# One hybrid decoder layer: token rows gathered in fp32 at 48 seats per expert, and 4 MB of expert 16 loaded before the expert loop

## What is computed

```python
exp_logits = ((xt @ w_expert).astype(jnp.float32) + b_expert.astype(jnp.float32)
              ).reshape(-1, N_GROUPS, EXPERTS_PER_GROUP)
sel_logits = jnp.take_along_axis(exp_logits, grp_idx[:, :, None], axis=1)[:, 0]
top_p, top_idx = lax.top_k(jax.nn.softmax(sel_logits, axis=-1), TOP_K)
...
for e in range(N_EXPERTS):
    he = jax.nn.silu(xt @ w1[e]) * (xt @ w3[e])
    y = y + combine[:, e:e + 1] * (he @ w2[e]).astype(jnp.float32)
```

## Time and profile before

| | us |
|---|---|
| median of 3 runs | 1478.21 |
| lowest, highest | 1477.36, 1479.08 |
| profiled execution, device time | 1476.32 |
| its span (first to last instruction) | 1474.5 |

### The profile page before, as it was taken

How to read it: one execution, slowest core, us unless ns; L and a number is a source line. 1 busy time by engine, 2 the same in 40 slices (tenths; PEclk the granted TensorE clock), 3 DMA queues, 4 the chain that set the end, 5 groups by cost and what they waited for, 6 DMA issues and landing times.

```text
span 1474.5 us, 20318 instructions
## 1 busy us (share of the span) xinstructions
PE 1355.0 (92%) x7740; PEld 834.6 (57%) x7740; DVE 612.2 (42%) x1136; ACT 440.0 (30%) x865; POOL 65.1 (4%) x63
## 2 busy tenths in 40 slices
PE   5999999999999798899999999899899889899885
PEld 3899999999988653343353353353353344335332
DVE  5977787778864611232223212212222122222223
ACT  5465655656654411111021011111111111111102
POOL 0012221022100000000000000000000000000000
PEclk9999999999999999999999999999999999999998
DMA  7565555555546759999999999999999999999994
GB/s 204 151 156 151 147 148 151 128 149 144 200 143 212 309 230 430 426 428 428 427 428 429 428 428 428 429 425 425 428 429 428 428 429 428 427 428 429 428 428 173
DMA packets 147064, 481.63 MB, mean 327 GB/s; under 512 B 11385, under 2 KB 112978, under 8 KB 121810
## 3 DMA queue, kind: packets, MB, share of 16 engines
q1 hardware_dynamic: 147026, 481.10, 83.5%
HBM read 478.96 MB, written 2.12 MB: 326 GB/s over the span
## 4 chain that ended last, share of the span: by engine, by line
PE 67%; DMA 24%; DVE 5%; ACT 2%; issue 1%; SPq 1%; DVEq 0%; ACTq 0%
PE bank L562 65%; DMA ew<-in_expert_w_dram 23%; PE bank L565 2%; DVE w_parts L1430 1%; ACT ew L1342 1%; DMA mixT<-in_x_dram 1%; SPq L529 0%; ACT fw_r L1269 0%; DVE ew L1469 0%; DVE fw L1889 0%; ACT fw L1009 0%; DVE fw_r L1750 0%; DVE fw L1390 0%; DVE fw L1940 0%; DVE ew L1897 0%
## 5 line engine op out<-in xcount | busy, mean ns | idle before, releaser
L562 PE MATMUL bank<-ew,hT 128*64 128x512 f32 (+1 forms) x1568 | 466.7, 602 | 39.5 <-DMA ew<-in_expert_w_dram 32.0
L562 PEld LDWEIGHTS bank<-ew,hT 128*64 128x64 f32 (+1 forms) x1568 | 157.1, 141 | 336.1 <-issue 335.9
L562 PE MATMUL bank<-act_parts,w_parts 128*128 128x256 f32 x2304 | 308.1, 288 | 1.7 <-DVE w_parts L1430 1.7
L562 PEld LDWEIGHTS bank<-act_parts,w_parts 128*128 128x128 f32 x2304 | 285.2, 191 | 2.9 <-issue 1.4
L562 PE MATMUL bank<-ew 128*64 128x512 f32 (+2 forms) x1120 | 248.8, 574 | 6.8 <-DVE ew L1899 6.8
L562 PE MATMUL bank<-mixT,hT 128*64 128x512 f32 x512 | 227.0, 596 | 0.0
L1897 DVE SCALAR_TENSOR_TENSOR ew<-ew,bank 128x256 f32<-128x256 f32 x32 | 13.5, 421 | 453.9 <-ACT ew L1344 453.9
L562 PEld LDWEIGHTS bank<-ew 128*64 128x64 f32 (+1 forms) x1120 | 84.8, 141 | 147.5 <-issue 137.2
L1430 DVE TENSOR_TENSOR w_parts<-fw,w_parts 128x2048 fp32r<-128x2048 f32 x64 | 147.8, 2313 | 31.5 <-ACT w_parts L1031 30.5
L1359 ACT ACTIVATE ye_r<-bank 64x512 fp32r<-64x512 f32 x128 | 68.8, 585 | 279.7 <-PE bank L562 278.9
L1342 ACT ACTIVATE ew<-bank,gs 128x512 f32<-128x512 f32 x32 | 22.0, 687 | 422.1 <-PE bank L562 422.1
(11 more groups left out here) (243 smaller groups left out, 1084.3 us busy)
## 6 DMA issues: line engine op xcount, KB each, us to landing
ew<-in_expert_w_dram SPq DMA_DIRECT2D x160, 2048.0 KB, 16.2
mixT<-in_expert_w_dram SPq DMA_DIRECT2D x32, 2048.0 KB, 18.6
fw<-in_w_in_dram SPq DMA_DIRECT2D x48, 1024.0 KB, 5.9
fw<-in_w_out_dram SPq DMA_DIRECT2D x16, 1024.0 KB, 5.0
mixT<-in_x_dram SPq DMA_DIRECT2D x1, 2048.0 KB, 7.4
fw<-in_x_dram SPq DMA_DIRECT2D x1, 2048.0 KB, 9.7
out_dram<-fw SPq DMA_DIRECT2D x4, 512.0 KB, 2.7
hT<-decay_rows SPq DMA_DIRECT2D x8, 192.0 KB, 5.8
```

Source lines behind the costliest of these rows:

```text
L562: return nc.tensor.matmul(o, l, r, start=start, stop=stop, skip_group_check=True)
```

## The change

**Gather.** The row split is gone. The gather reads the fp32 residual `x2` itself through a view (`xk`) whose 128 channels of a block lie 16 floats (64 bytes) apart, with 48 columns per expert: 16 x 2 = 32 fp32 products of 192 columns. The gathered rows lie in `seats`, 48 per expert; the up products still load 64 columns of it (the last only 48). Rounds would be needed from 49 tokens per expert on, before from 65. The one-hot columns beyond 48 are zeroed once by GpSimd. The first gather is cut 4 + 4 groups instead of 5 + 3, and expert j=0 waits for the gathered groups one by one. The experts' outputs are added into a copy `acc` of the residual, which ACT makes in four copies (`keep`), because `x2` is now read by every gather.

**Ahead.** Pieces 0 and 1 of expert 16 are loaded before the loop into four spare places (2 MB, 1 MB, 0.5 MB, 0.5 MB); in the loop SP skips these two loads, and the loop is written in two parts around expert 16.

**Order on PE.** The first half of `combine` moves ahead of the transposes of j=0 and j=2, and the gate columns ahead of those of j=3; DVE's additions move likewise. The router's weights and some small tiles move to other places.

```diff
-def build(nc, ins, out, slots=SLOTS):
+def build(nc, ins, out, slots=SEATS):
...
+        spare = sb("spare", [P, 1024])
+        R6 = Region(spare[:, :], 1024)
...
-        hn_hi = [fw_r[:, D:2 * D], fw_r[:, 2 * D:3 * D]]
-        hn_lo = [misc_r[:, 0:D], fw_r[:, 0:D]]
+        acc = fw[:, 0:2 * D].rearrange("p (t d) -> p t d", t=NT)
+        xk = x2.rearrange("q t (p k) -> q t k p", k=KD)
+        seats = hT[:, :, :].rearrange("p a b -> p (a b)")
+        XT = KD * QUAD * SEATS
+        ahead = [fw[:, 2 * D:4 * D], misc[:, 0:D], spare[:, :], seats[:, XT:XT + 1024]]
...
+        wfin = fw[:, 4 * D:5 * D]
+        rw = cst[:, C_BIG:C_BIG + KD * 36].rearrange("p (k n) -> p k n", k=KD)
+        rb = cst[:, C_BIG + KD * 36:C_BIG + KD * 36 + 36]
...
-                    sp.wait_ge(s_proj, NH * 6 + 7)
+                    sp.wait_ge(s_atm, NH * (LEVELS - 1))
+                    sp.wait_ge(s_aq, NH)
...
             load_expert(0, 0)
             load_expert(0, 1)
+            sp.wait_ge(s_y, NH)
+            sp.wait_ge(s_mix, 2 * NH)
+            sp.dma_start(ahead[1], expert_piece(AHEAD, 1)[:, 0:D]).then_inc(s_ahead, 16)
+            sp.dma_start(ahead[2], expert_piece(AHEAD, 1)[:, D:D + 1024]).then_inc(s_ahead, 16)
+            sp.wait_ge(s_proj, NH * 6 + 8)
+            sp.wait_ge(s_restD, NH * 6 + 15)
+            sp.dma_start(ahead[0], expert_piece(AHEAD, 0)).then_inc(s_ahead, 16)
             for piece in range(2, 6):
                 sp.wait_ge(s_proj, NH * 6 + min(12 + piece, 16))
                 load_expert(0, piece)
+            sp.wait_ge(s_lgt, NT)
+            sp.dma_start(ahead[3], expert_piece(AHEAD, 1)[:, D + 1024:]).then_inc(s_ahead, 16)
...
             with sp.Fori(0, rounds) as r:
-                with sp.Fori(1, NE) as e:
+                with sp.Fori(1, AHEAD) as e:
+                    for piece in range(6):
+                        sp.wait_ge(s_ed, (r * NE + e - 1) * 6 + piece + 1)
+                        load_expert(e, piece)
+                for piece in range(2):
+                    sp.wait_ge(s_ed, (r * NE + AHEAD - 1) * 6 + piece + 1)
+                    sp.nop().then_inc(s_ew[piece], 16)
+                for piece in range(2, 6):
+                    sp.wait_ge(s_ed, (r * NE + AHEAD - 1) * 6 + piece + 1)
+                    load_expert(AHEAD, piece)
+                with sp.Fori(AHEAD + 1, NE) as e:
                     for piece in range(6):
                         sp.wait_ge(s_ed, (r * NE + e - 1) * 6 + piece + 1)
                         load_expert(e, piece)
...
@@ -858,18 +888,15 @@
             mm(bank[5][:, 2 * NE:3 * NE], one, hot[:, 0:NE], True, False)
             mm(bank[5][:, 2 * NE:3 * NE], one, hot[:, NE:], False, True).then_inc(s_rank, 1)
 
...
-            pe.wait_ge(s_hnH, 2 * NT)
-            pe.wait_ge(s_hnL, 2 * NT)
...
+            seated = pick[:, :, :, 0:P].rearrange("p t a (b s) -> p t a b s", s=SLOTS)[:, :, :, :, 0:SEATS]
 
             def gather_group(o, g):
                 for c in range(2):
-                    for lo in range(2):
-                        for t in range(NT):
-                            k = 2 * g + c
-                            l = mm(o[:, c * T:(c + 1) * T], (hn_lo if lo else hn_hi)[t][:, k * P:(k + 1) * P],
-                                   pickr[:, t, :, 0:P], lo == 0 and t == 0, lo == 1 and t == NT - 1)
+                    for t in range(NT):
+                        l = mm(o[:, c * WIDE:(c + 1) * WIDE], xk[:, t, 2 * g + c, :], seated[:, t], t == 0, t == NT - 1)
                 l.then_inc(s_xg, 1)
...
+                pe.wait_ge(s_pz, 1)
                 pe.wait_ge(s_pick, n + 1)
                 pe.wait_ge(s_turn, r + 1)
-                for g in range(5):
+                for g in range(4):
                     gather_group(bank[FIRST[g]], g)
...
-                for g in range(5, 8):
+                for g in range(4, 8):
                     if g == 6:
                         pe.wait_ge(s_xeA, n * 4 + 1)
-                    else:
+                    elif g > 4:
                         pe.wait_ge(s_xeD, n * 4 + (1 if g == 5 else 2))
                     gather_group(bank[FIRST[g]], g)
                 pe.wait_ge(s_gq0, 1)
                 gate_slots()
 
-            def gather_next(n):
+            def gates_next(n):
 
                 pe.wait_ge(s_pick, n + 1)
                 for t in range(NT):
                     pe.wait_ge(s_add[t], n * 8 - 4)
                 gate_slots()
...
+            def gather_next(n):
+
                 for g in range(8):
                     if g >= 2:
                         pe.wait_ge(s_xeA if g % 2 else s_xeD, n * 4 + g // 2)
...
-            def combine(n, pair):
+            def combine(n, pair, t):
 
                 m = pe.snap(n * 2 + pair)
-                pe.wait_ge(s_placeT, n + 1)
-                pe.wait_ge(s_yeA, m * 8 + 8)
-                pe.wait_ge(s_yeD, m * 2 + 2)
-                for i in range(8):
+                if t == 0:
+                    pe.wait_ge(s_placeT, n + 1)
+                    pe.wait_ge(s_yeA, m * 8 + 8)
+                    pe.wait_ge(s_yeD, m * 2 + 2)
+                for i in range(t * 4, t * 4 + 4):
...
+            def quad(n, q, first, last, has_ahead=False):
...
-                        if j == 0:
-                            pe.wait_ge(s_xeA, n * 4 + 2 + 2 * half)
-                            pe.wait_ge(s_xeD, n * 4 + 2 + 2 * half)
                         for which in range(2):
                             pe.wait_ge(s_ew[half * 2 + which], e * 16 + 16)
+                        if has_ahead and j == 0 and half == 0:
+                            pe.wait_ge(s_ahead, 64)
                         for k in range(KD // 2):
+                            if j == 0 and k % 2 == 0:
+                                pe.wait_ge(s_xeA if k % 4 else s_xeD, n * 4 + 2 * half + k // 4 + 1)
+                            at = (half * 8 + k) * WIDE + j * SEATS
+                            rows = min(SLOTS, XT - at)
                             for which in range(2):
-                                l = mm(bank[2][which * 64:which * 64 + 64, :],
-                                       xT[:, half * 8 + k, j * SLOTS:(j + 1) * SLOTS],
-                                       ewp[half * 2 + which].rearrange("p (k n) -> p k n", n=FF)[:, k, :],
+                                l = mm(bank[2][which * 64:which * 64 + rows, :], seats[:, at:at + rows],
+                                       up_weights(half * 2 + which, k, has_ahead and j == 0),
                                        half == 0 and k == 0, half == 1 and k == KD // 2 - 1)
                                 if k == KD // 2 - 1:
...
+                    if j == 0 and not first:
+                        combine(pe.snap(n - 1), 1, 0)
+                    elif j == 2:
+                        combine(n, 0, 0)
+                    elif j == 3 and not last:
+                        gates_next(pe.snap(n + 1))
                     pe.wait_ge(s_hs, e + 1)
                     for k in range(FC):
                         l = tr(bank[3][:, k * P:(k + 1) * P], hs.rearrange("p (f k) -> p k f", k=FC)[:, k])
                     l.then_inc(s_HT, 1)
                     if j == 0 and not first:
-                        combine(pe.snap(n - 1), 1)
+                        combine(pe.snap(n - 1), 1, 1)
                     if j == 1:
                         places(n, first)
                     if j == 2:
-                        combine(n, 0)
+                        combine(n, 0, 1)
                     if j == 3 and not last:
                         gather_next(pe.snap(n + 1))
...
-                with pe.Fori(1, NQUAD - 1) as q:
+                with pe.Fori(1, AHEAD // QUAD) as q:
+                    quad(pe.snap(r * NQUAD + q), q, False, False)
+                quad(pe.snap(r * NQUAD + AHEAD // QUAD), AHEAD // QUAD, False, False, True)
+                with pe.Fori(AHEAD // QUAD + 1, NQUAD - 1) as q:
                     quad(pe.snap(r * NQUAD + q), q, False, False)
                 quad(pe.snap(r * NQUAD + (NQUAD - 1)), NQUAD - 1, False, True)
-                combine(pe.snap(r * NQUAD + (NQUAD - 1)), 1)
+                for t in range(NT):
+                    combine(pe.snap(r * NQUAD + (NQUAD - 1)), 1, t)
...
-            def high_rows(t, lo, hi):
-                act.activation(hn_hi[t].rearrange("q (k p) -> q k p", k=KD)[:, :, lo:hi],
-                               x2[:, t].rearrange("q (p k) -> q k p", k=KD)[:, :, lo:hi], ACT.Copy).then_inc(s_hnH, 1)
-
+            def keep(t, lo, hi):
+                act.activation(acc[:, t, lo:hi], x2[:, t, lo:hi], ACT.Copy)
...
-            act.wait_ge(s_restD, NH * 6 + 15)
-            high_rows(1, 0, 96)
+            act.wait_ge(s_restD, NH * 6 + 16)
+            for t in range(NT):
+                keep(t, 0, 3 * 512)
...
-                        l = act.activation(xT[:, 2 * g + c, :], bank[banks[g]][:, c * T:(c + 1) * T], ACT.Copy,
```

(36 more changed lines are left out.)

70 lines of the change are left out of this document (32 added, 38 removed).

## The result

| | us |
|---|---|
| kernel before, median of 4 runs beside it | 1477.78 |
| changed kernel, median of 4 runs | 1506.03 (1503.25 to 1508.53) |
| ratio, with its 95% interval | 1.0194 (1.018 to 1.0209) |
| profiled execution of the changed kernel, its span | 1508.53, 1506.7 |

The change costs 28 us. The forecast was no change, 1478 us, with a range of 1473 to 1500: the measured 1506 lies outside it. What the prediction called rival 1 (the stationary load at a 64-byte stride) is the mechanism, at a higher price than it was given.

What follows compares the result with a forecast made beforehand. The DMA queue was taken as the bound, so time is stream start, bytes and tail. Terms -9.8 + 6.8 + 2.6 - 0.5 = -0.9, plus 0.9 for lower clock: no change, 1478 us, range 1473 to 1500.

Steps and rivals of the forecast that it cites:

- rival 1: Gather's stationary load at a 64-byte stride: 0.21 to 0.225 us an instruction, +14 to +25 us, near 1496; chance 0.27.
- The gather: Each expert gather: 64 fp32 instructions at 0.16 to 0.17 us, 10.3 to 10.9 us against 8.6, +2.3, mostly covered.
- six quads: Under rival 1, gathers in six other quads: DMA queue idles 0.7 + 0.5, lower clock 1 to 2 more; 1.2 to 3 each.
- The hole: DMA queue near expert 16, short of two preloaded pieces: idle 6.3 us, then 0.5 before expert 17's piece 0; +6.8.
- The first gather: Expert 0's gather, before the unbroken stream: nothing covers it, 12.3 us with the lower clock against 9.7; +2.6.
- Ahead of the loop: Path to the round count: row split removed, partly offset by short compares and smaller one-hot writes; -0.5 us.
- the order around the transposes: PE at three places in a quad: 3.5 to 4 us more slack, none in the time while the queue is the bound.
- loads ahead of the loop: Expert 16's two pieces leave the stream, -9.8 us; loading them in idle DMA time before the loop costs nothing.

Runs made afterwards that it cites:

- the first probe: Changed kernel plus 128 extra fp32 products, results overwritten, at strides of 1 to 32 floats ahead of the gather for experts 16 to 19; no kernel time given.

## Why the prediction was wrong

**The step that failed first is "The gather".** "The floor set by loading 128 stationary columns is 1.87/16 = 0.117, which lies beneath 0.16": that row was of a contiguous load. At the 64-byte stride the load takes 0.21 to 0.22, and the columns (0.164, as worked out) vanish beneath it. The two bounds were both in the text, and the choice between them went by the wrong row: the `hs` transposes are PE's own and at a stride of 16 bytes, but they are transposes, and those do not pay. The rows of ACT and DVE, given less weight because they were other engines, said 1.8 to 1.9, and it was 0.222/0.117 = 1.9. The rule that the prediction quotes from the Trainium skill (SBUF — State Buffer, Specifications) was right for this load, and I weighed it down by a row of another operation.

**The price of rival 1 (+14 to +25) was too low**, mainly in one term: six quads at 1.2 to 3 us, which lost 2.3 to 5.1. Its hole, 6.8 + 3.6 = 10.4, was 12.6, and the tail's 1.6 was not in it; its first gather, +6.2, was right (+6.1). Two things are in the quads. Its formula had 13.5 + 14.2 = 27.7 against a queue of 27.9, so nearly no gap. But a queue that is nearly dry is slower already: behind the gather shown above the transfer is at 240 GB/s for 3 us though its share is 0.75, and once more when the next piece pair starts:

```profile
767.00:770.00 3.00, 3.00 (x18) 1.00 (x15) 0.00 (x0) 0.00 (x0) 0.00 (x0) 1.00 0.75 240
...
779.00:781.00 2.00, 2.00 (x12) 0.60 (x10) 0.00 (x0) 0.00 (x0) 0.00 (x0) 1.00 0.88 262
```

That is 1.3 + 0.8 us of this gather's 2.3. And in three of the six quads the lower clock fell on half 1 ahead of the gather, which delayed piece 4 by some 1.7 more (8.8 for 7.1, as in the tail):

```profile
860.00:865.00 5.00, 3.54 (x10) 1.34 (x12) 0.00 (x0) 0.00 (x0) 0.00 (x0) 0.70 1.02 436
```

Those three lost 4.0 to 5.1, the others 2.3 to 2.7.

**The hole (+6.8)** was right in kind and too small. With the gather as assumed it is 9.8: of it 6.2 behind the gather (991 to 998, predicted 6.3), but 2.0 more ahead of pieces 2 and 3 (979 to 982). Half 1 took 8.8 us at the lower clock, and the queue holds only 8.3 then; I had taken 7.1 and seen no gap. The rest is the slow return to rate. (The prediction's own last part, 3.5 + 7.1 less 9.8, is 0.8 and not 0.5.) With the 14.2 us gather the hole is 12.6. Of that an ordinary gather would have lost 2 to 5 anyway, so the two pieces' 9.8 us were lost, and no more than that.

**The first gather (+2.6)** is 15.8 - 9.7 = +6.1 with the stride, and 7.8 + 5.3 = 13.1 without, +3.4: the lower clock cost 2.6 where I took 1.7. **Ahead of the loop (-0.5)**: the gather starts at 516.07 against 515.69, so no gain shows; but between the traces of the variants without extra products it starts anywhere from 515.02 to 516.29, so 0.5 us can't be told.

**Right:** that the queue bounds the loop and the ledger is to be made from its start, bytes and idling; that 64 instructions at their columns' pace take 10.3 to 10.9 (10.49); that the order around the transposes brings 3.5 to 4 us of slack per quad (3.6) and nothing in the time; that loads ahead of the loop hide (expert 1's piece 2 is issued at 543.46 and 545.45 in two traces with them and at 544.46 without, the gather being contiguous in all three) and that a hole at expert 16 eats most of them, though it ate all. Even with the gather right, the sum would have been 1478 where 1484.3 was measured: hole, first gather, ordinary gathers and tail together some 6 us too low, in the main for leaving out what happens at the edges of a queue that is short.

## What to carry to other kernels

Before a stationary operand is read through a strided view, ask how many bytes lie from element to element (8 were nearly free here, 16 and more doubled the load of 4-byte elements), and take the price from a row of the same operation, since another one on the same engine may be exempt. Where a full DMA queue is the bound, bytes taken out of it are worth their time only where buffers come free fast enough: here nothing in front of the gather, the longest gap between two releases, and nearly all of it two experts further.

## What the runs showed that I had not expected

- fp32 and fp32r products: 0.111 to 0.116 us and 0.133 to 0.14 us per instruction for a load of 128 columns at strides of 1 and 2 floats, 0.21 to 0.23 and 0.23 to 0.25 from 4 floats on (to 32 and to 16; the fp32r run at 4 lay partly at the lower clock). fp32 transposes: 0.11 to 0.12 at every stride tried, 1, 2, 4, 8 and 16.
- PE ran products of 42 to 50 columns, and then some of 190, without a pause, and the granted clock was 0.50, 1.2 GHz, for the 38 us from 1122 to 1160 (the window shown with the first probe).
- After 9 us without a transfer the queue came back at 284 GB/s over the first 3 us:

```profile
1002.00:1011.00 9.00, 9.00 (x43) 6.14 (x44) 1.15 (x4) 1.46 (x4) 0.00 (x0) 1.00 0.00 0
1011.00:1014.00 3.00, 3.00 (x16) 1.01 (x14) 0.00 (x0) 0.04 (x1) 0.00 (x0) 1.00 0.83 284
```
